# A hybrid attention and S5 block on one core: the GLU multiplies y itself, its buffers change places, sigmoids wait for the product alone, and the loads of turned u come in three parts

## The chip, the cores and the metric

The kernel runs on 1 core of one Trainium2 chip. The metric is the time of one execution in device microseconds (us); lower is better. Engines are named as in the profile: PE (TensorE), DVE (VectorE), ACT (ScalarE), POOL (GpSimd), SP (SyncE, which here only issues DMAs). ACT issues DMAs too, on a queue of its own; their issues are rows of "SPq" and "ACTq".

## The reference, cut to what matters

```python
# x: (1, 2048, 1024); one layer, float32
h = rms_norm(x, norm_mix)
q, k, v, u, g = split(h @ w_in)                        # u: 512 wide, g: two gates of 1024
branch_a = window_attention(q, k, v, sinks, bias) @ w_attn_branch
y = gelu(Re(C scan(A, B u)) + D u)                     # S5: 32 groups of 16 channels, 64 states each
branch_b = (y * sigmoid(y @ w_glu + b_glu)) @ w_ssm_branch
x = x + (sigmoid(g_A) * branch_a + sigmoid(g_B) * branch_b) @ w_out
x = x + conv_ffn(rms_norm(x, norm_ffn))                # 1024 -> 2 x 2816 -> 1024, depthwise conv of width 3
return rms_norm(x, norm_final)
```

## The kernel before

The 2048 tokens are worked on in two blocks (`blk`) of T = 1024. In each block PE goes through projections, attention with gate products between its pieces, the S5 recurrence with gate products between its pairs of groups, the GLU, the two branch products and merge, the output projection, and the ConvFFN. Everything is written out by hand in raw form: every engine has its own program, and semaphores set the order between engines. A float32 product is made of three matmuls on a high and a low part (fp32r) of each operand (`three`, L497 to L499); a half of a GLU or branch product (128 outputs, 512 tokens, four blocks of 128 inputs) is 12 matmuls of 512 columns.

**Weights.** They come in units of 512 KB. SP loads each into one of two buffers `w_raw` (L572), POOL makes the high part (L793, a cast) and the low part (L797, a subtraction) into one of two rings `w_hi`, `w_lo`; POOL may start on a unit when PE has used the one two units before, SP may load into `w_raw` when POOL is done with it. Units 6 and 11 to 25 are gates (two halves each), 26 and 27 the GLU, 28 to 35 the branches, and then those of the output projection (`wo`), which have eight buffers of their own.

**Turned u.** The S5 part wants u with eight consecutive tokens turned onto the partitions. ACT stores u to HBM (`useq`, semaphore `u_st`), and SP loads it back into `ssT` with eight DMAs of 256 KB, one for each token of a step (`load_steps`, L753; rows of 128 elements, 512 bytes). PE waits for all eight before the S5 loop, that is, after the attention.

**Gate halves.** ACT takes each gate product from PSUM into one of two buffers `junk` and stores it to HBM from its own DMA queue (`gate_out`, `gate_store`, L1046). It takes the next product of the same parity only when that store has landed. In the attention, one iteration of ACT is: 8 exponentials of a tile (L1129), `gate_out`, the high part of the attention output, the copy of the transposed probabilities; what comes next on ACT stands behind a `gate_out` that waits. In iteration 3 ACT also issues three loads of S5 tables (L1112).

**GLU.** y is turned back through HBM into `yT`. ACT makes `yT_hi` (`y_high`), DVE `yT_lo` = yT - yT_hi (`y_low`, L1616), in place of `yT` (both stand at 112 KiB). PE makes 8 half products. For each half n: ACT makes the sigmoid `glu_s`, DVE adds `yT_hi` and `yT_lo` again (L1674), multiplies by the sigmoid (L1676, `glu_y`), ACT makes the high part `ybr_hi`, and DVE the low part `ybr_lo` (L1681). `glu_s` and `glu_y` have two buffers each. The sigmoid of half n waits until `ybr_lo` of half n-2 is there (`ybr_ready`). PE works on the attention half of the first branch product meanwhile and then waits for all eight `ybr_lo`.

## Time and profile before

| | |
|---|---|
| time, median of 3 runs | 2474.99 us (2473.34 to 2483.62) |
| profiled execution | 2474.55 us, span in the trace 2472.8 us |
| PE busy | 2417.0 us, 98% of the span |
| DVE, ACT, POOL busy | 1737.5, 746.4, 855.5 us |
| TensorE clock granted, mean | 0.992 |

Busy time of PE is modelled from the start of its matmuls; a matmul of 512 columns shows 0.39 us, and the next one starts 0.23 us after it when PE runs through. PEclk is the granted clock as a share of full speed: 1.00 is 2.4 GHz, 0.50 is 1.2 GHz. Times in rows are in us from the start of the span, and idle time before an instruction stands in square brackets with what ended it.

### The profile page before, as it was taken

To read this page: it belongs to the slowest core of one execution; us is meant where nothing else is said; L and a number is where in the kernel's file an instruction comes from. 1 tells how busy PE (TensorE), PEld (TensorE's weight loads), DVE (VectorE), ACT (ScalarE), POOL (GpSimd) and SP (SyncE) were. 2 spreads that over 40 slices of the span, in tenths; PEclk is the share of its full clock that TensorE was granted. 3 is DMA by queue.
4 is the path that set the end of the run, shared out by engine and by line. 5 is a ranking of instruction groups with operands and counts; after the bars stand their busy time and mean duration, and the time that the engine had idled before them with its cause. 6 is when DMAs were issued, how large, how long until landed. Compare 5 with 4: busy or idle time off the path is not lost.

```text
span 2472.8 us, 33390 instructions
## 1 busy us (share of the span) xinstructions
PE 2417.0 (98%) x11578; PEld 1980.7 (80%) x11578; DVE 1737.5 (70%) x2585; ACT 746.4 (30%) x1431; POOL 855.5 (35%) x689
## 2 busy tenths in 40 slices
PE   7999999999999999999999999999999999999997
PEld 6887777888788888788878877778878888888886
DVE  6964564546899999989750346466378888888896
ACT  4145113212333333332221341132133333333222
POOL 2421222450455555623232222235213333334231
PEclk9999999999999999999999999999999999999999
DMA  6266553351334334698522536534312222218863
GB/s 206 77 182 108 175 170 120 133 194 71 102 126 156 135 131 133 216 371 290 183 88 90 104 119 188 158 105 156 148 60 80 91 85 76 78 75 289 311 230 136
DMA packets 178279, 367.35 MB, mean 149 GB/s; under 512 B 22344, under 2 KB 60008, under 8 KB 178168
## 3 DMA queue, kind: packets, MB, share of 16 engines
q1 hardware_dynamic: 135568, 278.23, 34.7%
q10 hardware_dynamic: 42600, 87.64, 10.3%
q8 instruction: 70, 1.15, 0.2%
q14 instruction: 41, 0.34, 0.0%
HBM read 277.20 MB, written 88.60 MB: 148 GB/s over the span
## 4 chain that ended last, share of the span: by engine, by line
PE 90%; DVE 5%; DMA 2%; ACT 2%; issue 1%; POOL 0%; ACTq 0%; SPq 0%; DVEq 0%; POOLq 0%
PE ps L497 28%; PE ps L499 28%; PE ps L498 28%; DMA gates<-junk 1%; PE ps L2220 1%; PE ps L2222 1%; PE ps L2202 1%; DVE ybr_lo L1681 1%; PE ps L2026 1%; PE ps L2074 0%; PE ps L2159 0%; DVE glu_y L1676 0%; ACT ybr_hi L909 0%; DVE z L1809 0%; DVE act_lo L1842 0%
## 5 line engine op out<-in xcount | busy, mean ns | idle before, releaser
L839 POOL CAST slot_hi<-pair_raw 128x512 fp32r<-128x512 f32 x220 | 201.7, 924 | 394.4 <-PE ps L499 305.5
L497 PE MATMUL ps<-act_hi,w_hi 128*128 128x512 f32 x832 | 332.1, 399 | 1.5 <-issue 1.5
L499 PE MATMUL ps<-act_hi,w_lo 128*128 128x512 f32 x832 | 325.4, 391 | 0.0
L498 PE MATMUL ps<-act_lo,w_hi 128*128 128x512 f32 x832 | 324.6, 390 | 0.0
L793 POOL CAST w_hi<-w_raw 128x1024 fp32r<-128x1024 f32 x72 | 80.6, 1119 | 678.4 <-PE ps L499 668.8
L497 PE MATMUL ps<-act_hi,slot_hi 128*128 128x512 f32 x704 | 274.4, 390 | 1.8 <-DVE pre L1795 1.5
L499 PE MATMUL ps<-act_hi,slot_lo 128*128 128x512 f32 x704 | 274.0, 389 | 0.0
L498 PE MATMUL ps<-act_lo,slot_hi 128*128 128x512 f32 x704 | 273.9, 389 | 0.0
L497 PE MATMUL ps<-act_hi 128*128 128x512 f32 x616 | 242.0, 393 | 3.2 <-DVE act_lo L1846 3.2
L498 PE MATMUL ps<-act_lo,act_hi 128*128 128x512 f32 x616 | 240.9, 391 | 0.0
L499 PE MATMUL ps<-act_hi,act_lo 128*128 128x512 f32 x616 | 240.8, 391 | 0.0
L899 POOL CAST act_hi<-step_w 128x512 fp32r<-128x512 f32 x154 | 136.2, 911 | 292.4 <-PE ps L499 280.9
L497 PE MATMUL ps<-tw_hi,slot_hi 128*128 128x512 f32 x528 | 206.3, 391 | 1.6 <-ACT part L909 1.4
L499 PE MATMUL ps<-tw_hi,slot_lo 128*128 128x512 f32 x528 | 205.5, 389 | 0.0
L498 PE MATMUL ps<-tw_lo,slot_hi 128*128 128x512 f32 x528 | 205.5, 389 | 0.0
L1742 DVE TENSOR_TENSOR slot_lo<-pair_raw,slot_hi 128x512 fp32r<-128x512 f32 x220 | 184.0, 838 | 13.8 <-POOL slot_hi L839 12.8
L797 POOL TENSOR_TENSOR w_lo<-w_raw,w_hi 128x1024 fp32r<-128x1024 f32 x72 | 186.3, 2588 | 9.9 <-DVE xin L1447 4.3
L839 POOL CAST slot_hi<-sums 128x512 fp32r<-128x512 f32 x84 | 118.8, 1414 | 202.8 <-DVE sums L1722 102.6
L497 PEld LDWEIGHTS ps<-act_hi,w_hi 128*128 128x128 f32 x832 | 156.8, 188 | 35.8 <-issue 3.6
L499 PEld LDWEIGHTS ps<-act_hi,w_lo 128*128 128x128 f32 x832 | 156.7, 188 | 34.0
L498 PEld LDWEIGHTS ps<-act_lo,w_hi 128*128 128x128 f32 x832 | 157.0, 189 | 30.9
L909 ACT ACTIVATE act_hi<-step_f 128x512 fp32r<-128x512 f32 x154 | 89.0, 623 | 268.7 <-PE ps L499 173.0
(325 smaller groups left out, 4953.2 us busy)
## 6 DMA issues: line engine op xcount, KB each, us to landing
w_raw<-in_wu SPq DMA_DIRECT2D x88, 512.0 KB, 3.4
pair_raw<-in_wu SPq DMA_DIRECT2D x88, 512.0 KB, 4.1
step_f<-ff SPq DMA_DIRECT2D x88, 512.0 KB, 5.2
ff<-z SPq DMA_DIRECT2D x44, 512.0 KB, 2.6
gates<-junk ACTq DMA_DIRECT2D x64, 256.0 KB, 2.1
sig<-gates ACTq DMA_DIRECT2D x32, 512.0 KB, 5.3
tbl_o<-tables ACTq DMA_DIRECT2D x32, 384.0 KB, 3.6
step_w<-in_wu SPq DMA_DIRECT2D x22, 512.0 KB, 6.8
```

What stands on the lines that cost most here:

```text
L497: nc.tensor.matmul(out, lh, rh, start=first, stop=False, skip_group_check=onto)
L498: nc.tensor.matmul(out, lh, rl, start=False, stop=False, skip_group_check=onto)
L499: return nc.tensor.matmul(out, ll, rh, start=False, stop=last, skip_group_check=onto)
L793: nc.gpsimd.tensor_copy(hi, w_raw[b][:, :]).then_inc(hi_made, 1)
L797: nc.gpsimd.tensor_tensor(lo, w_raw[b][:, :], f(hi), ALU.subtract).then_inc(w_ready, 1)
L839: nc.gpsimd.tensor_copy(slot_hi[j][:, :, :], src).then_inc(slot_half[KIND[j]], 1)
L899: nc.gpsimd.tensor_copy(d_hi[slot][part], weight_of(t, n)).then_inc(d_half, 1)
L909: ins = nc.scalar.activation(out, in_, kw.pop("func", ACT.Identity), **kw)
L1681: tt(by_step(ybr_lo, q), glu_y[b][:, :].rearrange("p (t n) -> p t n", t=4), f(by_step(ybr_hi, q)), ALU.subtract).then_inc(ybr_ready, 1)
L1742: tt(slot_lo[j][:, :, :], src, f(slot_hi[j][:, :, :]), ALU.subtract).then_inc(slot_ready[KIND[j]], 1)
L2026: return nc.tensor.transpose(ps[:, x_bank(blk, h, k), q * P:(q + 1) * P], src, ident[:, :])
L2202: ins = mm(ps[SS * g:SS * g + SS, s_bank[m % 2], ri * P:(ri + 1) * P], tbl_r[m % NR][:, TB_W + ri * P + SS * g:TB_W + ri * P + SS * g + SS ...
```

## The change

It has three parts.

**The GLU multiplies y itself.** `yT_lo` moves from 112 to 160 KiB, so that `yT` stays whole; the addition L1674 is gone, and the multiplication reads `yT`. `ybr_lo` moves from 160 to 112 KiB, over `yT`; before the first `ybr_lo` of a pair of halves is written, DVE waits until both products of this pair are made (`glu_yr`). At 160 to 176 KiB stand tables of the S5 loop, so all eight `y_low` now stand behind the loop, where four did before; two of the four `y_low` calls stood in the loop, at its steps 9 and 13. The buffers of `wo` are taken in another order.

**Sigmoids.** From n = 2 on, ACT's sigmoid of half n waits for the product of half n-2 (`glu_yr`) and not for its `ybr_lo`.

**Loads of turned u.** The eight DMAs are issued as three, three and two, with two weight units between the first and the second part and two between the second and the third.

```diff
@@ buffers
-        yT_lo = at("yT_lo", 112, [4, T], F32R)
+        yT_lo = at("yT_lo", 160, [4, T], F32R)
         ybr_hi = at("ybr_hi", 144, [4, T], F32R)
-        ybr_lo = at("ybr_lo", 160, [4, T], F32R)
+        ybr_lo = at("ybr_lo", 112, [4, T], F32R)
...
         wo = [(at(f"wo_hi{i}", a, [D], F32R), at(f"wo_lo{i}", a + 4, [D], F32R))
-              for i, a in enumerate((96, 104, 112, 120, 144, 152, 160, 168))]
+              for i, a in enumerate((96, 104, 160, 168, 112, 120, 144, 152))]
@@ SP
-                def load_steps():
+                def load_steps(lo, hi):
                     rows = A["useq"].rearrange("(g c) (t n) -> t c g n", c=SC, t=STEP)
                     sp.wait_ge(u_st, 16 * 4 * (blk + 1))
-                    for t in range(STEP):
+                    for t in range(lo, hi):
                         sp.dma_start(ssT[SC * t:SC * t + SC, :, :], rows[t]).then_inc(steps_in, 16)
-                load_weights(first, (U_GATE + 6) // 2)
-                load_steps()
+                if blk:
+                    load_weights(first, (U_GATE + 4) // 2)
+                load_steps(0, 3)
+                load_weights((U_GATE + 4) // 2, (U_GATE + 6) // 2)
...
-                load_weights((U_GATE + 6) // 2, (U_GATE + 14) // 2)
+                load_steps(3, 6)
+                load_weights((U_GATE + 6) // 2, (U_GATE + 8) // 2)
+                load_steps(6, STEP)
+                load_weights((U_GATE + 8) // 2, (U_GATE + 14) // 2)
                 load_y(0)
@@ ACT
                         if n >= 2:
-                            act.wait_ge(ybr_ready, blk * 8 + n - 1)
+                            act.wait_ge(glu_yr, blk * 8 + n - 1)
                         copy(glu_s[n % 2][:, :], ps[:, 2 + n % 4, :], glu_sig, 1, func=ACT.Sigmoid, bias=bglu[:, n // 2:n // 2 + 1])
@@ DVE
-                    if n in (9, 13):
-                        y_low((n - 9) // 4)
...
-                y_low(2)
-                y_low(3)
-
-                dve.wait_ge(y_ready, (blk + 1) * 8)
+                dve.wait_ge(y_done, (blk + 1) * PAIRS)
+                for kt in range(4):
+                    y_low(kt)
+
                 for n in range(9):
                     if n < 8:
...
                         if n >= 2:
                             dve.wait_ge(ybr_ready, blk * 8 + n - 1)
-                        link(tt(glu_y[b][:, :], f(yT_hi[:, m, cols]), f(yT_lo[:, m, cols]), ALU.add))
                         dve.wait_ge(glu_sig, blk * 8 + n + 1)
-                        tt(glu_y[b][:, :], glu_y[b][:, :], glu_s[b][:, :], ALU.mult).then_inc(glu_yr, 1)
+                        tt(glu_y[b][:, :], yT[:, m, cols], glu_s[b][:, :], ALU.mult).then_inc(glu_yr, 1)
                     if n >= 1:
                         q = n - 1
+                        b = q % 2
+                        if q % 2 == 0:
+                            dve.wait_ge(glu_yr, blk * 8 + min(q + 2, 8))
                         dve.wait_ge(glu_hi, blk * 8 + q + 1)
                         tt(by_step(ybr_lo, q), ...
```

On PE a wait for all eight `ybr_lo` stands before each of the two halves of the first S5 branch product, where it stood before the first alone.

**DVE, block 0, from the end of the S5 loop into the GLU** (`yT_lo` low parts of y, `glu_y` products, `ybr_lo` low parts of the branch's input). Before:

```order
L1616 TENSOR_TENSOR yT_lo<-yT,yT_hi 128x512 x4
L1674 TENSOR_TENSOR glu_y_99<-yT_hi,yT_lo 128x512
L1676 TENSOR_TENSOR glu_y_99<-glu_y_99,glu_s_97 128x512
L1674 TENSOR_TENSOR glu_y_100<-yT_hi,yT_lo 128x512
L1676 TENSOR_TENSOR glu_y_100<-glu_y_100,glu_s_98 128x512
L1681 TENSOR_TENSOR ybr_lo<-glu_y_99,ybr_hi 128x4x128
L1674 TENSOR_TENSOR glu_y_99<-yT_hi,yT_lo 128x512
L1676 TENSOR_TENSOR glu_y_99<-glu_y_99,glu_s_97 128x512
L1681 TENSOR_TENSOR ybr_lo<-glu_y_100,ybr_hi 128x4x128
```

The same place in the changed kernel:

```order
L1621 TENSOR_TENSOR yT_lo<-yT,yT_hi 128x512 x8
L1678 TENSOR_TENSOR glu_y_99<-yT,glu_s_97 128x512
L1678 TENSOR_TENSOR glu_y_100<-yT,glu_s_98 128x512
L1685 TENSOR_TENSOR ybr_lo<-glu_y_99,ybr_hi 128x4x128
L1678 TENSOR_TENSOR glu_y_99<-yT,glu_s_97 128x512
L1685 TENSOR_TENSOR ybr_lo<-glu_y_100,ybr_hi 128x4x128
```

Eight additions are gone, and eight `yT_lo` stand in a row instead of four.

**SP, block 0, from the last store of S5 tables to the first load of y** (`ssT` turned u, `w_raw` weight units). Before:

```order
L588 DMA tables<-set_kmat 16x16x16
L745 UNCONDITIONAL_BRANCH
L572 DMA w_raw_176<-in_wu 128x1024
L572 DMA w_raw_177<-in_wu 128x1024
L745 REGISTER_ALU
L745 COMPARE_AND_BRANCH
L753 DMA ssT<-useq 16x32x128 x8
```

In the changed kernel:

```order
L588 DMA tables<-set_kmat 16x16x16
L753 DMA ssT<-useq 16x32x128 x3
L745 UNCONDITIONAL_BRANCH
L572 DMA w_raw_176<-in_wu 128x1024
L572 DMA w_raw_177<-in_wu 128x1024
L745 REGISTER_ALU
L745 COMPARE_AND_BRANCH
L753 DMA ssT<-useq 16x32x128 x3
L745 UNCONDITIONAL_BRANCH
L572 DMA w_raw_176<-in_wu 128x1024
L572 DMA w_raw_177<-in_wu 128x1024
L745 REGISTER_ALU
L745 COMPARE_AND_BRANCH
L753 DMA ssT<-useq 16x32x128 x2
```

The first three loads of u now stand ahead of weight units 14 and 15, the next three right behind them, and the last two behind units 16 and 17. In block 1 the order is the same, with units 0 to 13 ahead of it.

## Rows read from the trace of the kernel before

**Rows 1.** The page, engine busy times and the chain by engine.
```profile
PE 2417.0 (98%) x11578; PEld 1980.7 (80%) x11578; DVE 1737.5 (70%) x2585; ACT 746.4 (30%) x1431; POOL 855.5 (35%) x689
...
PE 90%; DVE 5%; DMA 2%; ACT 2%; issue 1%; POOL 0%; ACTq 0%; SPq 0%; DVEq 0%; POOLq 0%
```

**Rows 2.** Stretches: us, busy (instructions) of PE, PEld, DVE, ACT, POOL; PEclk; DMA share; GB/s.
```profile
205.00:212.00 7.00, 4.99 (x42) 3.97 (x39) 1.60 (x3) 2.05 (x9) 0.00 (x0) 0.80 1.06 250
212.00:222.00 10.00, 10.00 (x52) 7.58 (x51) 5.93 (x13) 5.90 (x21) 2.45 (x2) 0.80 0.14 51
426.00:430.00 4.00, 3.96 (x9) 3.14 (x10) 1.12 (x1) 1.35 (x2) 0.00 (x0) 0.50 0.72 261
430.00:434.00 4.00, 4.00 (x17) 3.23 (x16) 0.00 (x0) 1.35 (x2) 0.00 (x0) 0.87 0.00 1
654.00:662.00 8.00, 6.48 (x29) 5.04 (x28) 7.76 (x9) 3.38 (x7) 5.07 (x6) 1.00 0.16 63
```

**Rows 3.** PE in order of time, block 0, GLU: start, us, [idle before <-releaser].
```profile
393.68 0.39 PE L497 MATMUL ps<-yT_hi,w_hi 128*128 128x512 f32 x1
...
415.44 0.39 PE L497 MATMUL ps<-attn_hi,w_hi 128*128 128x512 f32 x1
...
426.05 0.79 PE L497 MATMUL ps<-ybr_hi,w_hi 128*128 128x512 f32 x1 [5.01 <-DVE ybr_lo L1681]
```

**Rows 4.** PE in order of time, block 1, the same wait.
```profile
1641.67 0.80 PE L497 MATMUL ps<-ybr_hi,w_hi 128*128 128x512 f32 x1 [5.04 <-DVE ybr_lo L1681]
```

**Rows 5.** DVE in order of time, block 0, GLU.
```profile
381.43 1.29 DVE L1616 TENSOR_TENSOR yT_lo<-yT,yT_hi 128x512 fp32r<-128x512 f32 x2 [13.02 <-ACT yT_hi L909]
...
411.58 0.69 DVE L1676 TENSOR_TENSOR glu_y<-glu_y,glu_s 128x512 f32<-128x512 f32 x1 [0.16 <-ACT glu_s L909]
...
415.69 1.16 DVE L1681 TENSOR_TENSOR ybr_lo<-glu_y,ybr_hi 128x512 fp32r<-128x512 f32 x1 [0.32 <-ACT ybr_hi L909]
416.88 1.40 DVE L1674 TENSOR_TENSOR glu_y<-yT_hi,yT_lo 128x512 f32<-128x512 f32 x1
418.31 2.77 DVE L1676 TENSOR_TENSOR glu_y<-glu_y,glu_s 128x512 f32<-128x512 f32 x1
421.00 1.07 DVE L1681 TENSOR_TENSOR ybr_lo<-glu_y,ybr_hi 128x512 fp32r<-128x512 f32 x1
```

**Rows 6.** ACT in order of time, block 0, GLU.
```profile
416.94 0.69 ACT L909 ACTIVATE glu_s<-ps,bglu 128x512 f32<-128x512 f32 x1 [1.28 <-DVE ybr_lo L1681]
417.52 1.20 ACT L909 ACTIVATE ybr_hi<-glu_y 128x512 fp32r<-128x512 f32 x1
```

**Rows 7.** POOL in order of time, block 0, GLU.
```profile
415.80 1.93 POOL L793 CAST w_hi<-w_raw 128x1024 fp32r<-128x1024 f32 x1 [6.71 <-PE ps L499]
417.81 2.72 POOL L797 TENSOR_TENSOR w_lo<-w_raw,w_hi 128x1024 fp32r<-128x1024 f32 x1
```

**Rows 8.** The chain in order of time, block 0, attention: start, us, what.
```profile
186.00 13.41 DMA gates<-junk
...
201.49 1.10 ACTq L1112
```

**Rows 9.** PE in order of time, block 0, attention.
```profile
207.70 1.10 PE L2159 MATMUL ps<-ident,logit 128*128 128x128 f32 x8 [2.01 <-DVE logit L1594]
```

**Rows 10.** PE in order of time, block 1, attention.
```profile
1425.98 0.77 PE L2159 MATMUL ps<-ident,logit 128*128 128x128 f32 x5 [0.83 <-DVE logit L1594]
```

**Rows 11.** Waits of ACT, block 0, attention: us in total, times, longest.
```profile
ACT junk L909 <- DMA gates<-junk: 15.7, 3, 7.3
```

**Rows 12.** SP's DMA queue up to the late store, block 0.
```profile
181.84 0.86 SPq L572 DMA_DIRECT2D w_raw<-in_wu  x2
182.94 4.92 SPq L753 DMA_DIRECT2D ssT<-useq  x5
```

**Rows 13.** Tile ssT, block 1: DMA issues (ns, first and last start), time to landing.
```profile
L753 SPq DMA_DIRECT2D ssT<-useq x8: 330/1182/2417, 1401.7 to 1410.4; - x8
...
DMA to landing us min/median/max: 6.8/13.8/15.9
```

More of the change, by code:

```diff
@@ L1673, in _ @@
                             dve.wait_ge(ybr_ready, blk * 8 + n - 1)
-                        link(tt(glu_y[b][:, :], f(yT_hi[:, m, cols]), f(yT_lo[:, m, cols]), ALU.add))
                         dve.wait_ge(glu_sig, blk * 8 + n + 1)
-                        tt(glu_y[b][:, :], glu_y[b][:, :], glu_s[b][:, :], ALU.mult).then_inc(glu_yr, 1)
+                        tt(glu_y[b][:, :], yT[:, m, cols], glu_s[b][:, :], ALU.mult).then_inc(glu_yr, 1)
                     if n >= 1:
                         q = n - 1
-                        b, m, cols = q % 2, q // 2, slice((q % 2) * HALF, (q % 2 + 1) * HALF)
+                        b = q % 2
+                        if q % 2 == 0:
+                            dve.wait_ge(glu_yr, blk * 8 + min(q + 2, 8))
                         dve.wait_ge(glu_hi, blk * 8 + q + 1)
@@ L2244, in _ @@
                     for j in range(2):
-                        if m == 0 and j:
-                            pe.wait_ge(ybr_ready, (blk + 1) * 8)
                         for h in range(2):
+                            if m == 0 and j:
+                                pe.wait_ge(ybr_ready, (blk + 1) * 8)
                             ins = unit_half(4 * (m % 2) + 2 * j + h, m % 2, h, (attn_hi, ybr_hi)[j], (attn_lo, ybr_lo)[j], 4 * j, 4)
```

## The prediction

> **What bounds the kernel now.** I read the page first. PE is busy for 98% of the span and the chain that ended last runs over PE for 90% of it [rows 1]: only time in which PE stands still, or runs at the low clock, can be won. PE's idle time is 2472.8 - 2417.0 = 55.8 us in all. So I looked for PE's waits in the two places that the diff touches, and then for the clock behind them.
>
> In the GLU, PE makes eight half products from 393.68 to 415.44, 2.72 us each, works on the attention half of the first branch product, and stands still for 5.01 us until the last `ybr_lo`, at 426.05 [rows 3]. Block 1 has the same wait, 5.04 us [rows 4]. Behind it the granted clock is 0.50, that is 1.2 GHz, for the 4 us from 426 and at a mean of 0.87 over the next 4 us, which makes 4 + 1.04 = 5.0 us at half speed [rows 2]: 2.5 us of work lost beyond the wait itself. For block 1 I take the same.
>
> In the attention of block 0, a gate store issued at 186.00 lands after 13.41 us [rows 8]; ACT wants its buffer 7.3 us before that [rows 11], and everything behind it on ACT is late. PE waits 2.01 us for the probabilities at 207.70 [rows 9]. The mean clock is 0.80 over the 7 us from 205 and 0.80 over the 10 us from 212 [rows 2], so 2.8 + 4.0 = 6.8 us at half speed, 3.4 us lost. Block 1 has a wait of 0.83 us there [rows 10].
>
> **The GLU, step by step.** Why is the last `ybr_lo` late? The products would allow a half each 2.72 us. Before, the sigmoid of half n waited for `ybr_lo` of half n-2, so sigmoid, product, high part and low part stood in a ring. When POOL works on a weight unit, DVE's share stretches: the addition at 416.88 takes 1.40 and the product at 418.31 takes 2.77 us, where the same product takes 0.69 at 411.58 [rows 5]; POOL's cast and subtraction run at 415.80 and 417.81 [rows 7]. This happens twice in a block, and the ring hands each delay on. Now the sigmoid waits only for PE and for a product two halves back, and DVE has one operation of 0.69 us less per half. Per half DVE needs 0.69 + 1.2 = 1.9 and ACT 0.69 + 1.20 = 1.9 us [rows 5, 6], under PE's 2.72. So the chain should run at PE's pace, and only the last two halves show.
>
> The last product ends just before 415.80, since POOL's cast waits for it too [rows 7]. By my reckoning with the durations above: `ybr_lo` of half 5 from about 414.8 to 415.9; sigmoid of half 7 from 415.7 to 416.4; POOL's cast, behind that `ybr_lo`, to about 416.9; the product of half 7 from then to 417.6; high part of half 6 to 417.5 and of half 7 to 418.9; POOL's subtraction, asked for at 417.0 and so ahead of the next `ybr_lo`, from 417.6 to 419.9 (its 2.72 less the 0.4 in which it was held up); `ybr_lo` of half 6 to 421.0, of half 7 to 422.1. PE starts at 422.2, not at 426.05: 3.85 us per block, and a wait of 422.2 - 421.04 = 1.2 us remains. Another wait of about this size, 1.52 us near 655 (8.00 - 6.48 busy), leaves the clock at 1.00 [rows 2], so I take the 2.5 us as won too. Per block 3.85 + 2.5 = 6.35, for two blocks **12.7 us**. Bounds: with no POOL work in the way the wait vanishes, 5.0 + 2.5 = 7.5 per block, 15.0; with the clock falling all the same 3.85 per block, 7.7.
>
> The remaining wait is where a rule speaks against the change. The rows show it first: the product at 418.31 ends at 421.08, 0.55 us after POOL's subtraction (417.81 + 2.72 = 420.53) [rows 5, 7], as if it had not begun before. The Trainium skill (SBUF — State Buffer, Who interferes with whom) says that a DVE instruction with two inputs in SBUF contends with a GpSimd instruction that reads SBUF, and that the one issued second is blocked entirely. By that rule the new product, which still has two SBUF inputs, is blocked as the old one was, and the wait of 1.2 us stays; if instead both only slowed down, the last `ybr_lo` would come near 421 and the sum would be 15 instead of 12.7.
>
> **The moved low parts.** All eight `yT_lo` now follow the S5 loop; two make 1.29 us [rows 5], so the four that leave the loop are 2.6 us. DVE is idle for 13.02 us before 381.43 [rows 5], in which they fit, and the last two wait for y to come back from HBM as before. Cost nothing; without that cover 2.6 us per block. The wait for the pair's two products, on DVE itself, comes after an instruction that has just been issued there; the first `ybr_lo` already waits for `ybr_hi`. It is at nothing, with 0.16 us per pair at most, by the wait for the own result in [rows 5]. Other buffers for `wo` and PE's doubled wait move nothing: the second wait is for a number already reached.
>
> **The loads of u.** In block 1 a part takes (1410.4 + 15.9 - 1401.7 - 6.8) / 7 = 2.5 us when the parts are queued (first landing to last) [rows 13]. The gate store of block 0 lands 13.41 us after issue, five parts (12.7 us) and a bit [rows 8], and five parts had been handed over or begun by then (182.94 + 4.92) [rows 12]: a store lands when what was issued ahead of it has gone through. So what counts is what SP has issued by the time ACT stores.
>
> Block 0: the two weight units were issued at 181.84, right ahead of the parts [rows 12]. Now three parts go first, then the units, then three parts without any wait between. At 186.00 about the same is in front of the store, and it lands near 199.4 again. But two of eight parts, 5 us, are gone behind it, and with them the 1.10 us for which ACT's exponentials waited on the issue of a table load into a full queue [rows 8]. PE's wait becomes 2.01 - 1.1 = 0.9 us, like the 0.83 of block 1, whose mean clock the page does not show falling. Gain 1.1 + 3.4 = **4.5 us**; bounds 0 (wait and clock as before) and 5.4 (all gone).
>
> Block 1: SP can load unit 15 only when POOL is done with unit 13, an iteration after unit 14, so the first two parts are truly apart. A store has three parts in front of it instead of five, lands about 5 us earlier, and the 0.83 us go: **0.8 us**, bounds 0 and 0.8. The first part comes an iteration earlier; the last two parts still come iterations before PE asks for them. Behind `u_st` on SP stand weight units 14 and 15 now; POOL can take unit 14 only when PE has used unit 12, so a delay of 3 x 2.5 = 7.5 us lies within its slack.
>
> **Sum.** 12.7 + 4.5 + 0.8 = 18.0 us. The profiled execution took 2474.55, 1.8 above its span and 0.4 below the median of the runs shown: 2474.55 - 18.0 = 2456.5, and against the median 2457.0 us, which I forecast (0.7% faster). About 0.5%, 12.4 us, is what a measurement of this kernel can tell from no change: the border is at 2462.6.
>
> **Rivals.**
> - *No wait remains in the GLU.* DVE's last two low parts slip in ahead of POOL, or POOL's subtraction comes later. For it: the order at 417.6 is a matter of 0.1 us. Time 2457.0 - 2.3 = 2454.7. Chance 0.12.
> - *The clock falls behind the remaining wait.* The row at 655 speaks against it, but at 207.70 a wait of 2.01 us was enough [rows 2, 9], and 1.2 lies between. One block 2459.5, both 2462.0. Chance 0.14.
> - *Block 0's attention keeps its wait.* Three parts, two units, three parts back to back are nearly the old burst. Then 4.5 is missing: 2461.5. Chance 0.15; together with a clock that falls, 2466.5, 0.05.
> - *The GLU change does not do what it says*: the chain was bound by POOL, and the low part of half 7 still ends near 426, because each of the twelve operations in between yields to POOL. Against it: ACT stood idle 1.28 us before the sigmoid at 416.94, and what ended that was `ybr_lo` [rows 6], the very wait that is taken out. 2457.0 + 12.7 = 2469.7. Chance 0.04.
> - *Slower*: each of the three parts holds up a gate store, in each block. Before, one store per block is that late. If every part makes a store land 13.4 us after issue, as in [rows 8], and PE pays 2.01 + 3.4 = 5.4 us each time, six such places cost 32.4 against the 6.2 of before: 26 more, less 12.7 won in the GLU, 2475.0 + 26.2 - 12.7 = 2488.5. Its point: a store may take 13.4 - 7.3 = 6.1 us before ACT is late, and PE has 7.3 + 1.1 - 2.01 = 6.4 us of slack behind ACT [rows 8, 9, 11], so it costs from 12.5 us on; three parts and a weight unit are below 10. Chance 0.03.
>
> **How the numbers follow.** The forecast as written has 0.47. Range 2452 to 2467: below it lies only both upper bounds and more (15.0 + 6.2 = 21.2, 2453.8, with a microsecond or two for the spread of runs), above it the last two rivals. Faster by over 0.5%: forecast, first two rivals and nearly all of the third, 0.83. Within 0.5%: part of the third, third with second, the fourth, 0.13. Slower 0.04.
>
> **What would show it.** PE's idle before the first product with `ybr_hi` at 1.2 us instead of 5.01 in both blocks, with PEclk 1.00 behind it; sigmoids 2.7 us apart, waiting for PE; product and `ybr_lo` stretched where POOL subtracts. In the attention, a gate store that still takes 13 us in block 0 and about 8 in block 1, and a wait of PE under 1 us in place of 2.01, with no 0.80 in PEclk. It is wrong if PE waits elsewhere: for `y_ready` at the head of the GLU, for `steps_in` ahead of the S5 loop, or for probabilities in another iteration.

## The result and the profile after

The changed kernel takes **2454.79 us** (median of 4 runs, 2454.64 to 2455.12); the kernel before, beside it on the same chip, 2474.16 (4 runs, 2470.70 to 2483.62). The ratio is 0.9923, 95% interval 0.9905 to 0.9941: 19.4 us or 0.8% faster. The forecast was 2457.0 us, range 2452 to 2467. The profiled execution took 2454.71 us with a span of 2452.9 us, 19.9 less than before, and the mean granted clock rose from 0.992 to 0.998.

The page, engine busy times and the chain by engine; they answer to [rows 1]:

```profile
PE 2408.1 (98%) x11578; PEld 1973.6 (80%) x11578; DVE 1726.3 (70%) x2569; ACT 747.8 (30%) x1431; POOL 855.0 (35%) x689
...
PE 92%; DVE 4%; DMA 1%; issue 1%; ACT 1%; SPq 0%; POOL 0%; DVEq 0%; POOLq 0%; ACTq 0%
```

PE's busy time fell by 8.9 us with the same number of matmuls; they ran less at the low clock, as the stretches below show. The other 11.0 us of the span are idle time of PE that is gone (55.8 to 44.8).

PE in order of time. Block 0: the attention's transposed probabilities, which waited at 207.70 [rows 9], the first matmul of the GLU, and the first product with `ybr_hi` [rows 3]. The last two rows are block 1's, an iteration of the attention and the same product.

```profile
205.54 1.09 PE L2163 MATMUL ps<-ident,logit 128*128 128x128 f32 x8
...
388.36 0.39 PE L497 MATMUL ps<-yT_hi,w_hi 128*128 128x512 f32 x1
...
416.43 0.50 PE L497 MATMUL ps<-ybr_hi,w_hi 128*128 128x512 f32 x1 [0.71 <-DVE ybr_lo L1685]
...
1413.05 0.66 PE L2163 MATMUL ps<-ident,logit 128*128 128x128 f32 x4
...
1623.98 0.50 PE L497 MATMUL ps<-ybr_hi,w_hi 128*128 128x512 f32 x1 [0.75 <-DVE ybr_lo L1685]
```

Block 1's attention and GLU had 0.83 and 5.04 us of wait before [rows 4, 10]. Set beside the rows of before, they say where the time went. The GLU of block 0 begins 393.68 - 388.36 = 5.3 us earlier: all of that was won in the attention. Its product with `ybr_hi` is 426.05 - 416.43 = 9.6 us earlier, 4.3 more, which is 5.01 - 0.71. In block 1 it is 1641.67 - 1623.98 = 17.7 us earlier. The stretches that answer to [rows 2], with the same columns, and one in the ConvFFN:

```profile
205.00:212.00 7.00, 7.00 (x55) 5.65 (x52) 4.21 (x12) 5.02 (x20) 0.00 (x0) 1.00 0.12 44
212.00:222.00 10.00, 10.00 (x68) 7.83 (x67) 5.88 (x13) 5.40 (x20) 3.39 (x2) 1.00 0.41 97
416.00:420.00 4.00, 3.57 (x16) 2.96 (x17) 1.51 (x2) 0.00 (x0) 0.00 (x0) 1.00 0.84 280
420.00:424.00 4.00, 4.00 (x19) 3.34 (x18) 1.69 (x2) 2.12 (x2) 1.50 (x2) 1.00 0.22 87
1038.00:1046.00 8.00, 8.00 (x30) 6.41 (x29) 8.00 (x12) 1.05 (x2) 2.56 (x2) 0.79 0.55 178
```

The clock stays at 1.00 (2.4 GHz) where it was 0.80, 0.80, 0.50 and 0.87. The last row is the one place in the middle of the program where it still falls.

**DVE in the GLU, block 0** (answers to [rows 5]):

```profile
372.21 2.50 DVE L1621 TENSOR_TENSOR yT_lo<-yT,yT_hi 128x512 fp32r<-128x512 f32 x4 [9.11 <-PE ps L2226]
...
385.30 1.29 DVE L1621 TENSOR_TENSOR yT_lo<-yT,yT_hi 128x512 fp32r<-128x512 f32 x2 [8.09 <-ACT yT_hi L914]
...
401.32 3.21 DVE L1685 TENSOR_TENSOR ybr_lo<-glu_y,ybr_hi 128x512 fp32r<-128x512 f32 x1
404.57 0.69 DVE L1678 TENSOR_TENSOR glu_y<-yT,glu_s 128x512 f32<-128x512 f32 x1
405.18 1.19 DVE L1685 TENSOR_TENSOR ybr_lo<-glu_y,ybr_hi 128x512 fp32r<-128x512 f32 x1
...
409.42 1.18 DVE L1685 TENSOR_TENSOR ybr_lo<-glu_y,ybr_hi 128x512 fp32r<-128x512 f32 x1 [0.34 <-ACT ybr_hi L914]
411.11 0.95 DVE L1678 TENSOR_TENSOR glu_y<-yT,glu_s 128x512 f32<-128x512 f32 x1 [0.51 <-ACT glu_s L914]
412.21 4.17 DVE L1685 TENSOR_TENSOR ybr_lo<-glu_y,ybr_hi 128x512 fp32r<-128x512 f32 x2
```

**POOL, the same stretch** (answers to [rows 7]):

```profile
400.78 2.73 POOL L802 TENSOR_TENSOR w_lo<-w_raw,w_hi 128x1024 fp32r<-128x1024 f32 x1
...
411.60 2.75 POOL L802 TENSOR_TENSOR w_lo<-w_raw,w_hi 128x1024 fp32r<-128x1024 f32 x1
```

The stretched `ybr_lo` at 401.32 ends at 404.53 instead of after 1.2 us, and POOL's subtraction beside it at 403.51. Now the delay is not handed on: DVE runs without a gap from 404.57, two operations of 0.69 and 1.19 us per half against PE's 2.72, and by 409.42 it is waiting for ACT again. In the last stretch two low parts that take 1.2 us each take 4.17: the first of them 3.18 us, to 415.39, which is 1.04 us behind the end of POOL's subtraction. PE's remaining 0.71 us of wait comes from there. DVE's idle time in front of the low parts of y (9.11 and 8.09 us) shows that four more of them cost nothing.

**ACT, the same stretch** (answers to [rows 6]):

```profile
404.88 0.69 ACT L914 ACTIVATE glu_s<-ps,bglu 128x512 f32<-128x512 f32 x1 [0.94 <-PE ps L499]
...
407.60 0.69 ACT L914 ACTIVATE glu_s<-ps,bglu 128x512 f32<-128x512 f32 x1 [0.95 <-PE ps L499]
```

Sigmoids stand 2.72 us apart, PE's pace, and what they wait for is PE and no longer `ybr_lo`.

**The attention.** SP's queue in block 0 (answers to [rows 12]), then the landing of the gate store of 185.9 (answers to [rows 8]), then ACT's waits, in us in total, times and longest (answers to [rows 11]):

```profile
181.53 1.52 SPq L753 DMA_DIRECT2D ssT<-useq  x3
183.17 0.89 SPq L572 DMA_DIRECT2D w_raw<-in_wu  x2
184.31 2.63 SPq L753 DMA_DIRECT2D ssT<-useq  x3
...
218.28 0.85 SPq L753 DMA_DIRECT2D ssT<-useq  x2
```

```profile
L1051 ACTq DMA_DIRECT2D gates<-junk x1: 326/326/326, 185.9 to 185.9; - x1
...
DMA to landing us min/median/max: 10.5/10.5/10.5
```

```profile
ACT junk L914 <- DMA gates<-junk: 7.8, 2, 4.4
```

The store lands after 10.5 us and not after 13.41, so ACT's longest wait for it is 4.4 us instead of 7.3, and PE has nothing to wait for. Six loads and two weight units are handed over in a row, at least as much as in the burst of before up to that time (two units and, by 187.9, five loads [rows 12]), only in another order.

### The profile page after: what moved, and what is told of

Read it like the earlier page. It is cut to its first block, busy times and chain, and to the rows that moved or that the text cites. A ratio compares the mean times of both kernels' runs of the same rounds, so it can differ in the third digit from the quotient of the medians.

```text
span 2452.9 us, 33368 instructions
## 1 busy us (share of the span) xinstructions
PE 2408.1 (98%) x11578; PEld 1973.6 (80%) x11578; DVE 1726.3 (70%) x2569; ACT 747.8 (30%) x1431; POOL 855.0 (35%) x689
## 3 DMA queue, kind: packets, MB, share of 16 engines
q8 instruction: 70, 1.15, 0.2%
## 4 chain that ended last, share of the span: by engine, by line
PE 92%; DVE 4%; DMA 1%; issue 1%; ACT 1%; SPq 0%; POOL 0%; DVEq 0%; POOLq 0%; ACTq 0%
PE ps L497 29%; PE ps L499 28%; PE ps L498 28%; PE ps L2224 1%; PE ps L2226 1%; PE ps L2206 1%; PE ps L2174 1%; PE ps L2163 1%; PE ps L2030 1%; DVE act_lo L1846 1%; DMA step_w<-tw 1%; PE ps L2078 0%; DVE act_lo L1850 0%; PE ps L2154 0%; DVE z L1813 0%
## 5 line engine op out<-in xcount | busy, mean ns | idle before, releaser
L1746 DVE TENSOR_TENSOR slot_lo<-pair_raw,slot_hi 128x512 fp32r<-128x512 f32 x220 | 184.0, 838 | 13.4 <-POOL slot_hi L844 12.4
```

Source lines behind the costliest of these rows:

```text
L1746: tt(slot_lo[j][:, :, :], src, f(slot_hi[j][:, :, :]), ALU.subtract).then_inc(slot_ready[KIND[j]], 1)
```

## The experiments

The expectations name theories by letter. A is the prediction's account where nothing else is said; B is the rival of that run; C and D, in the last two, are two accounts of when a store on ACT's queue lands beside SP's loads: after a certain number of SP's DMAs (C), or when all bytes handed over ahead of it have gone through (D).

**1. The loads in parts alone.** The kernel before, with nothing but the new `load_steps`:

```diff
-                load_weights(first, (U_GATE + 6) // 2)
-                load_steps()
+                if blk:
+                    load_weights(first, (U_GATE + 4) // 2)
+                load_steps(0, 3)
+                load_weights((U_GATE + 4) // 2, (U_GATE + 6) // 2)
...
-                load_weights((U_GATE + 6) // 2, (U_GATE + 14) // 2)
+                load_steps(3, 6)
+                load_weights((U_GATE + 6) // 2, (U_GATE + 8) // 2)
+                load_steps(6, STEP)
+                load_weights((U_GATE + 8) // 2, (U_GATE + 14) // 2)
```

> The kernel before with the loads of turned u in three parts, and nothing else of the change. Theory A (the gains are won place by place and add up): the comparison of the two traces gives 5.3 us in block 0's attention and 1.35 us in block 1's, so about 6.6 us less than before, near 2467.5 us; PE's waits of 5.0 us in the GLU stay, and no wait over 0.5 us is left in either attention. Rival B (the stores are quicker in the changed kernel only because other work around them moved): within 2 us of before, with a gate store of 13 us in block 0.

Measured 2467.70 us (10 runs, 2466.79 to 2469.48) against 2474.41 for before, ratio 0.9964 (0.9950 to 0.9978): 6.7 us. The store of 186 lands after 10.7 us, PE has no wait in either attention, and both waits of the GLU stand (5.05 and 5.02 us).

**2. The GLU and the sigmoids alone.** The changed kernel with the eight loads in one burst at their old place.

```diff
-                if blk:
-                    load_weights(first, (U_GATE + 4) // 2)
-                load_steps(0, 3)
-                load_weights((U_GATE + 4) // 2, (U_GATE + 6) // 2)
+                load_weights(first, (U_GATE + 6) // 2)
+                load_steps(0, STEP)
...
-                load_steps(3, 6)
-                load_weights((U_GATE + 6) // 2, (U_GATE + 8) // 2)
-                load_steps(6, STEP)
-                load_weights((U_GATE + 8) // 2, (U_GATE + 14) // 2)
+                load_weights((U_GATE + 6) // 2, (U_GATE + 14) // 2)
```

> The changed kernel with the eight loads of turned u in one piece, at their old place. Theory A: the 13.0 us of the two GLUs stay and the 6.6 us of the attention are given back: 2461.4 us; PE waits 0.7 us ahead of the first S5 branch product and 2.0 us for the probabilities of block 0 with the low clock behind it. Rival B (the low clock in the attention came from somewhere else): about 2456 us.

Measured 2461.67 us (9 runs, 2456.32 to 2468.17), ratio 0.9949 (0.9929 to 0.9969): 12.7 us. The GLU's waits are 0.73 and 0.72 us; the store takes 13.8 us, and PE waits for probabilities again, 1.42 us and in the next iteration 4.30:

```profile
207.04 1.09 PE L2158 MATMUL ps<-ident,logit 128*128 128x128 f32 x8 [1.42 <-DVE logit L1594]
...
220.76 1.97 PE L2158 MATMUL ps<-ident,logit 128*128 128x128 f32 x8 [4.30 <-DVE logit L1594]
```

The two halves of the change add up in the medians: 6.7 + 12.7 = 19.4 us, the whole. Their intervals are some 3 and 5 us wide to either side, so this is no close test, and place by place it is not what was expected. The profiled execution of this kernel (2465.67 us, 4 above its median) loses some 10 us to the changed kernel in block 0's attention, not 5.3, and nothing in block 1's: although the burst is there, with stores that land after 11.0 and 9.7 us, PE has no wait.

**3. The old wait of the sigmoid in the changed kernel.**

```diff
-                            act.wait_ge(glu_yr, blk * 8 + n - 1)
+                            act.wait_ge(ybr_ready, blk * 8 + n - 1)
```

> The changed kernel, but the sigmoid of half n waits for the low part of half n-2, as before. Theory A (the ring sigmoid, high part of the half before, low part, next sigmoid set the pace; the addition was hidden behind the sigmoid): steps of 0.69 + 1.1 + 1.18 + about 0.1 = 3.07 us again, PE waits 3 to 5 us in each block and the clock falls behind it: 2454.8 + 2 x (3 to 4.3 + 2.4) = 2465.6 to 2468.2 us. Rival B (what is won comes from the addition that is gone and from what POOL no longer stretches): steps near 2.7 us and under 2 us of waiting, below 2458 us.

Measured 2466.11 us (10 runs, 2465.23 to 2467.13), ratio 0.9964 (0.9948 to 0.9981). PE, ahead of the product with `ybr_hi`, and ACT's sigmoids before it:

```profile
419.51 0.80 PE L497 MATMUL ps<-ybr_hi,w_hi 128*128 128x512 f32 x1 [4.39 <-DVE ybr_lo L1685]
```

```profile
404.46 0.69 ACT L914 ACTIVATE glu_s<-ps,bglu 128x512 f32<-128x512 f32 x1 [3.08 <-DVE ybr_lo L1685]
...
407.58 0.69 ACT L914 ACTIVATE glu_s<-ps,bglu 128x512 f32<-128x512 f32 x1 [1.32 <-DVE ybr_lo L1685]
...
410.71 0.69 ACT L914 ACTIVATE glu_s<-ps,bglu 128x512 f32<-128x512 f32 x1 [1.36 <-DVE ybr_lo L1685]
...
415.55 0.69 ACT L914 ACTIVATE glu_s<-ps,bglu 128x512 f32<-128x512 f32 x1 [3.05 <-DVE ybr_lo L1685]
```

This is theory A, with both waits at 4.39 us. With the ring closed again, a lighter DVE hardly helps: after POOL's first unit the sigmoids follow at 3.12 and 3.13 us, slower than PE's 2.72, so what was lost is never caught up, and the second unit adds to it.

**4. The new wait of the sigmoid in the kernel before**, with its addition left in.

```diff
-                            act.wait_ge(ybr_ready, blk * 8 + n - 1)
+                            act.wait_ge(glu_yr, blk * 8 + n - 1)
```

> The kernel before with one edit: the sigmoid of half n waits for the product of half n-2. DVE still adds y, 0.69 + 0.69 + 1.18 us and about 0.3 of waits for its own results per half, 2.86, a little over PE's 2.72, and POOL stretches an addition and a product twice per block. Theory A: the wait shrinks from 5.0 to 2 to 3.5 us per block; the clock falls all the same if the wait is 2 us or more: 2474.2 - 2 x (1.5 to 3) = 2468.2 to 2471.2 us, and some 5 us less if the clock holds. Rival B (the wait alone does nothing without the addition gone): within 1 us of before.

Measured 2472.59 us (10 runs, 2465.19 to 2483.90), ratio 0.9983 (0.9961 to 1.0005): no change that can be told. The waits of the GLU are 3.78 and 3.81 us, over the 2 to 3.5 of theory A and under the 5 us that stay by rival B, and the clock still falls behind them. DVE shows why:

```profile
409.07 1.49 DVE L1674 TENSOR_TENSOR glu_y<-yT_hi,yT_lo 128x512 f32<-128x512 f32 x1
410.59 2.78 DVE L1676 TENSOR_TENSOR glu_y<-glu_y,glu_s 128x512 f32<-128x512 f32 x1
413.29 1.17 DVE L1681 TENSOR_TENSOR ybr_lo<-glu_y,ybr_hi 128x512 fp32r<-128x512 f32 x1
414.50 0.69 DVE L1674 TENSOR_TENSOR glu_y<-yT_hi,yT_lo 128x512 f32<-128x512 f32 x1
415.22 0.69 DVE L1676 TENSOR_TENSOR glu_y<-glu_y,glu_s 128x512 f32<-128x512 f32 x1
...
421.64 3.38 DVE L1681 TENSOR_TENSOR ybr_lo<-glu_y,ybr_hi 128x512 fp32r<-128x512 f32 x1
```

The ring is open, but three operations take 0.69 + 0.69 + 1.17 = 2.55 us per half, so DVE wins back only some 0.2 us per half on PE and is still late when the second unit of POOL stretches it again. Either edit alone leaves 4.4 or 3.8 us of wait; the two together leave 0.7. Block 0's attention has the program of before here, and yet its waits are others, 0.66 us at 206.31 and then this one, with the clock at a mean of 0.57 over 218 to 228:

```profile
219.50 1.97 PE L2159 MATMUL ps<-ident,logit 128*128 128x128 f32 x8 [3.77 <-DVE logit L1594]
```

That costs this execution 4 us more in the attention than the profiled one of before.

**5. POOL's second unit later.** The changed kernel, in which POOL takes the unit after the first branch unit only when all eight `ybr_lo` are there. Its loop is cut off at this unit:

```diff
-                with pool.Fori(1 if blk == 0 else 0, U_OUT // 2) as i:
+                with pool.Fori(1 if blk == 0 else 0, U_AB // 2) as i:
                     for b in range(2):
                         ring(i * 2 + (r0 + b), i + h0, i * 2 + (u0 + b), b)
+                for u in range(U_AB, U_OUT):
+                    if u == U_AB + 1:
+                        pool.wait_ge(ybr_ready, (blk + 1) * 8)
+                    ring(r0 + u, h0 + u // 2, u0 + u, u % 2)
```

> The changed kernel, but POOL makes the parts of the second branch unit only when all eight low parts are there, so that it reads no SBUF beside the last low parts. Theory A (the wait of 0.7 us is what POOL's subtraction adds to the low part of half 6, which takes about 3 us there instead of 1.18): the last two low parts take 2.1 us instead of 4.17, PE does not wait ahead of the first S5 branch product, the unit is ready at about +3.6 us, before PE wants it at +5.4: 2 x 0.7 = 1.4 us less than the changed kernel, 2453.4 us. Rival B (the last low parts are late for the steps ahead of them): the same wait, and the same time within 0.3 us; or the unit comes too late and PE waits there instead, 2455 to 2458 us.

Measured **2452.35 us** (6 runs, 2451.82 to 2453.05) against 2474.19 for before, ratio 0.9919 (0.9906 to 0.9933). Its slowest run is 1.6 us below the changed kernel's fastest (2454.64), and both stand beside equal medians of before (2474.16 and 2474.19); but they were not run side by side. DVE, then POOL:

```profile
411.88 2.26 DVE L1689 TENSOR_TENSOR ybr_lo<-glu_y,ybr_hi 128x512 fp32r<-128x512 f32 x2 [0.39 <-ACT ybr_hi L918]
```

```profile
414.33 1.04 POOL L798 CAST w_hi<-w_raw 128x1024 fp32r<-128x1024 f32 x1 [11.20 <-DVE ybr_lo L1689]
415.45 2.41 POOL L802 TENSOR_TENSOR w_lo<-w_raw,w_hi 128x1024 fp32r<-128x1024 f32 x1
```

The last two `ybr_lo` take 2.26 us instead of 4.17, and PE goes from its attention half at 415.02 to the product with `ybr_hi` at 415.25 without a wait. POOL has the unit ready at 417.9. The gain is 2.4 us where 1.4 was expected. Set instruction by instruction beside the changed kernel it is 1.01 and 1.05 us at the two products: the expectation counted the idle time of 0.7 alone, but the matmul behind the wait starts 1.10 us after the one before it instead of 0.23, and the next one 0.1 us late. The edit delays POOL's cast as well as its subtraction; what the run shows is that POOL's work on this unit makes the wait. This is the fastest kernel of the study.

**6. The parts later**: three loads behind units 14 and 15, three behind 16 and 17, two behind 18 and 19.

```diff
-                if blk:
-                    load_weights(first, (U_GATE + 4) // 2)
+                load_weights(first, (U_GATE + 6) // 2)
                 load_steps(0, 3)
-                load_weights((U_GATE + 4) // 2, (U_GATE + 6) // 2)
...
-                load_steps(3, 6)
                 load_weights((U_GATE + 6) // 2, (U_GATE + 8) // 2)
+                load_steps(3, 6)
+                load_weights((U_GATE + 8) // 2, (U_GATE + 10) // 2)
                 load_steps(6, STEP)
-                load_weights((U_GATE + 8) // 2, (U_GATE + 14) // 2)
+                load_weights((U_GATE + 10) // 2, (U_GATE + 14) // 2)
```

> The changed kernel, with the three parts one pair of weight units later (units 14 and 15 first, then three loads; units 16 and 17, three; 18 and 19, two). Theory A (a store takes as long as what was issued ahead of it and right behind it on SP's queue): block 0's store lands after some 8 us instead of 10.6, block 1's as now; PE has no wait there already: the same time within 1 us. Rival B: the last part now comes too late for the S5 loop, or collides with the loads of S5 tables, and PE waits at the loop's head: 2456 to 2462 us.

Measured 2484.69 us (4 runs, 2484.14 to 2486.64), ratio 1.0052 (1.0034 to 1.0070): slower than before, and 30 us slower than the changed kernel. Rival B had the place right and the price, at most 7 us, much too low. SP's queue and PE at the head of the S5 loop:

```profile
218.34 1.85 SPq L753 DMA_DIRECT2D ssT<-useq  x3
236.19 15.26 SPq L572 DMA_DIRECT2D w_raw<-in_wu  x2
251.66 0.85 SPq L753 DMA_DIRECT2D ssT<-useq  x2
```

```profile
261.20 1.12 PE L2205 MATMUL ps<-ssT,tbl_r 128*64 128x128 f32 x8 [12.82 <-issue]
```

SP can load unit 19 only when POOL gives its buffer free, at 251.0; the last two loads of u stand behind it, while PE has finished the attention at 248.4. PE stands still for 12.82 us, 13.15 in block 1, and runs at a mean clock of 0.69 for the 8 us behind. The store of 186, with only three loads behind the two units, lands after 9.9 us, which wins nothing more.

**7. All eight loads at the early place**, ahead of units 14 and 15.

```diff
-                load_steps(0, 3)
+                load_steps(0, STEP)
...
-                load_steps(3, 6)
-                load_weights((U_GATE + 6) // 2, (U_GATE + 8) // 2)
-                load_steps(6, STEP)
-                load_weights((U_GATE + 8) // 2, (U_GATE + 14) // 2)
+                load_weights((U_GATE + 6) // 2, (U_GATE + 14) // 2)
```

> The changed kernel, with all eight loads at the place of its first part, ahead of units 14 and 15. It tells the place from the splitting. Theory A (what counts is the number of loads in a burst beside a store): in block 0 the burst is as long as before and a store takes 13 us, PE waits 1 to 2 us with the low clock behind it, 5.3 us back; in block 1 the burst is one iteration earlier and costs 0.8 to 5 us: 2460 to 2465 us. Rival B (the earlier place alone wins it): the time of the changed kernel within 1 us.

Measured 2469.16 us (10 runs, 2464.98 to 2473.11), ratio 0.9982 (0.9971 to 0.9994). The store takes 14.3 us, and PE waits 3.29 us in block 0 and 3.19 us in block 1, more than theory A gave, whose range ended at 2465. The early place alone is worse than the old one: experiment 2 had a ratio of 0.9949, at most 0.9969.

**8. Six and two**: units 14 and 15, six loads, units 16 and 17, two loads.

```diff
-                if blk:
-                    load_weights(first, (U_GATE + 4) // 2)
-                load_steps(0, 3)
-                load_weights((U_GATE + 4) // 2, (U_GATE + 6) // 2)
+                load_weights(first, (U_GATE + 6) // 2)
+                load_steps(0, 6)
...
-                load_steps(3, 6)
                 load_weights((U_GATE + 6) // 2, (U_GATE + 8) // 2)
```

> The changed kernel, with six loads at the old place behind units 14 and 15 and the last two behind units 16 and 17. In block 0 the burst has the same six loads and two units as in the changed kernel, in another order. Theory A (only the two loads that are gone from the burst count in block 0): its store takes 10 to 11 us as in the changed kernel and PE does not wait; in block 1 the burst has six loads instead of three, its store some 11 us, PE waits at most 0.3 us: 2454.8 to 2456 us. Rival B (the units between the loads let the store through): the store takes 13 us in block 0, PE waits, 2458 to 2461 us.

Measured 2459.27 us (4 runs, 2456.36 to 2462.39), ratio 0.9951 (0.9932 to 0.9970). In block 0 SP hands over the same eight DMAs as the changed kernel, the two units first instead of in the middle, and the store takes 13.6 us and not 10.5:

```profile
L1048 ACTq DMA_DIRECT2D gates<-junk x1: 326/326/326, 186.0 to 186.0; - x1
...
DMA to landing us min/median/max: 13.6/13.6/13.6
```

PE waits 1.91 us for it, and this time the clock stays at 1.00:

```profile
205.00:212.00 7.00, 5.09 (x46) 4.00 (x43) 3.84 (x9) 5.20 (x21) 0.00 (x0) 1.00 0.32 121
```

Theory A, which gave 10 to 11 us, falls with this run, and rival B holds in landing, wait and time. What differs from the changed kernel up to the store is the order alone.

**9. Halved loads**: the kernel of experiment 2 with each load of u cut in two DMAs of 128 KB (PE waits for sixteen).

```diff
-                        sp.dma_start(ssT[SC * t:SC * t + SC, :, :], rows[t]).then_inc(steps_in, 16)
+                        for g in range(0, SG, SG // 2):
+                            sp.dma_start(ssT[SC * t:SC * t + SC, g:g + SG // 2, :], rows[t][:, g:g + SG // 2]).then_inc(steps_in, 16)
...
-                pe.wait_ge(steps_in, 16 * STEP * (blk + 1))
+                pe.wait_ge(steps_in, 16 * 2 * STEP * (blk + 1))
```

> Eight loads of turned u in one burst at the old place (as in e2_glu_alone), each cut into two DMAs of 128 KB over half of the groups: 16 DMAs, the same bytes and rows. In e2_glu_alone the store at 185.9 took 13.8 us and PE waited 1.42 us behind it. Theory C (a gate store gets one turn of service for each DMA of SP's queue and needs about five turns, so that it matters how long SP's DMAs are): the store lands after some 7 to 9 us, PE does not wait for probabilities, and the time is that of the changed kernel or 1 us above it, 2455 to 2457 us. Theory D (a store lands when the bytes ahead of it have landed, however they are cut): 13 to 14 us, PE waits 1 to 2 us as in e2_glu_alone, 2460 to 2463 us.

Measured 2454.94 us (4 runs, 2454.49 to 2463.08), ratio 0.9931 (0.9904 to 0.9958). The burst has the same place and the same bytes, and the store lands after 10.3 us instead of 13.8; PE has no wait in the attention. The time is the one of theory C, but the landing is neither its 7 to 9 us nor the 13 to 14 of theory D.

**10. Three and five**: three loads, units 14 and 15, the other five in one.

```diff
-                load_steps(3, 6)
-                load_weights((U_GATE + 6) // 2, (U_GATE + 8) // 2)
-                load_steps(6, STEP)
-                load_weights((U_GATE + 8) // 2, (U_GATE + 14) // 2)
+                load_steps(3, STEP)
+                load_weights((U_GATE + 6) // 2, (U_GATE + 14) // 2)
```

> The changed kernel, but the last two loads of turned u join the second part: three, units 14 and 15, five. In block 0 this is the burst of before with the two units behind the third load instead of ahead of the first. Theory C (turns: two of the store's five turns fall on weight units, which are quicker than loads of u): the store at 185.9 lands after 10 to 11 us as in the changed kernel (e8_six_then_two, with the units in front, took 13.6), and PE waits less than 0.7 us in block 0. Theory D (what is ahead or beside it in bytes): 13 us as in e8_six_then_two, and a wait of 1.5 to 2 us. In block 1 both expect a store of 11 to 13 us behind five loads and at most 0.9 us of waiting. Time 2455 to 2457 us by C, 2458 to 2462 us by D.

Measured 2456.04 us (4 runs, 2454.09 to 2457.52) against 2475.88, ratio 0.9924 (0.9902 to 0.9946). The store lands after 10.8 us although all eight loads are handed over in a row:

```profile
L1049 ACTq DMA_DIRECT2D gates<-junk x1: 326/326/326, 186.0 to 186.0; - x1
...
DMA to landing us min/median/max: 10.8/10.8/10.8
```

That is theory C's landing. In block 0 the units between the loads do nearly all of it; the third part adds little. In block 1 a wait of 0.70 us is left at 1414.22, which the changed kernel doesn't have.

## Why the prediction was right, and where it was not

**The GLU: right in mechanism and size.** 4.3 us of wait went per block (5.01 to 0.71, 5.04 to 0.75). Set instruction by instruction beside that of before, PE's program gains another 2.3 us (block 0) and 2.1 us (block 1) in the 7 us behind the wait, where the clock was low: 13.0 us where 12.7 was forecast. That the ring handed on each of POOL's two delays, and that both edits are needed to break it, is shown by experiments 3 and 4. The prediction named both edits, but not that neither does much alone: DVE must not only be let go, it must have time to catch up between POOL's two units (1.9 of 2.72 us per half against 2.55).

**The remaining wait: right in cause, somewhat too large.** Forecast 1.2 us, measured 0.71 and 0.75. With the 5.32 us added by which this execution is ahead, the sigmoid of half 7 (415.64) and POOL's cast (to 416.84) came as reckoned. The product of half 7 and the subtraction ended about 0.2 us sooner each (at 417.38 and 419.67 instead of 417.6 and 419.9), and the two low parts took another 0.2 less, to 421.70 instead of 422.1. That POOL's work on the unit is the cause is shown by experiment 5; that it is the subtraction is read from the times. The low parts at 401.32 and 412.21 end 1.02 and 1.04 us behind the subtraction that they were issued beside; undisturbed they take 1.15 to 1.2, as if they had begun only then. Had both engines gone at half speed, an estimate from that duration gives 2.4 us for such a low part, where 3.21 and 3.18 were measured. This agrees with the rule of the Trainium skill (SBUF — State Buffer, Who interferes with whom) that the prediction weighed: the one issued second is blocked, not slowed.

**The clock behind the remaining wait: right.** 1.00 behind 0.71 and 0.75 us. The rival in which it falls gives 2459.5 and more. The time alone could not tell the forecast from the first rival, no wait in the GLU: its 2454.7 is the measured time to 0.1 us, and yet the wait is there. It is luck that they meet; the microseconds came from the attention.

**The low parts of y and the other edits at nothing: right.** DVE idles 9.11 and 8.09 us in front of them, and PE shows no new wait at the head of the GLU.

**The attention of block 0: the gain is right within a microsecond, one step is wrong.** Forecast 4.5, measured 5.3: all of the wait of 2.01 us and of the 3.4 us of clock, within 0.1, which is about the upper bound of 5.4. All of this is two executions; experiments 2 and 4 show that the burst costs more in others. The step that failed is "At 186.00 about the same is in front of the store, and it lands near 199.4 again." The store of 185.9 landed after 10.5 us, at 196.4. So the wait went wholly, where 0.9 us was to stay. The step before it, that a store lands when what was issued ahead has gone through, was drawn from one row and doesn't hold: experiments 8 and 10 move the same DMAs past each other and get 13.6 and 10.8 us, and experiment 9 changes only how they are cut and gets 10.3. The slack that the prediction worked out for its slowest rival, that PE pays from a landing of about 12.5 us on, does fit block 0: at 10.8 us and less PE waits 0.35 us at most, at 13.2 and more it waits in each run. The landings of this one store:

| in front, from 181.5 on | store of 186 lands after |
|---|---|
| units, eight loads (before; experiments 2, 4) | 13.4; 13.8, 13.2 us |
| eight loads, units (7) | 14.3 |
| units, six loads (8) | 13.6 |
| three loads, units, five loads (10) | 10.8 |
| three loads, units, three loads (changed; 1, 3, 5) | 10.5; 10.7, 10.3, 10.6 |
| units, three loads (6) | 9.9 |
| units, sixteen halved loads (9) | 10.3 |

What is shown is that order and cut of SP's DMAs decide, at equal bytes. How they do is open. Theory C, a turn for each of SP's DMAs, gave experiments 9 and 10 the right direction; theory D, bytes, fails in both. The packets of the two queues (q1 is SP's, q10 ACT's; packets, MB, share of the 16 engines) say more. From 186 to 194, before, where ACT's queue has no row, and then in the changed kernel:

```profile
q1 hardware_dynamic: 1752, 0.96, 124.8%
```

```profile
q1 hardware_dynamic: 1114, 1.46, 104.8%
q10 hardware_dynamic: 138, 0.25, 8.3%
```

So the store does not go slowly beside the loads: it starts late, and then goes fast. Its first packet moves 8.7 us after its issue before the change, 6.8 in the changed kernel, 5.7 in experiment 9 and 11.0 in experiment 7; its last one starts 1.9 to 4.3 us behind the first in all runs. Between issue and first packet SP's queue moves 3.8, 3.0, 5.0 (halves) and 4.3 of its DMAs, or 1.0, 1.3, 0.7 and 1.1 MB: neither a fixed number of DMAs nor of bytes fits. In the runs without units between the loads the store starts when all but a part of one load (0.1 to 0.7 of it) of what was handed over ahead of it has moved, nearly as the prediction's step has it. In the changed kernel it overtakes two loads that were handed over ahead of it, behind the units. Why it does so there, no run shows.

**The attention of block 1: right in the number, the cause only in part shown.** 0.8 forecast, all of the wait of 0.83 us gone; PE gained 1.35 us there, of which a second wait of 0.40 us at 1435.82 is a part. The stores land after at most 8.0 us instead of 13.4, as forecast (about 5 us earlier). But PE has no wait in block 1 in the profiles of experiments 2 and 4 either, which keep the burst and have stores of 11.0 and 11.1 us. So the wait of before comes and goes with the same loads, and what the parts are worth here is less sure than the two profiles make it look.

**Sum.** 13.0 + 5.3 + 1.35 = 19.65, and 0.2 net from the ConvFFN: its low stretch of clock near 1050 is shorter (1.3 us won), and a wait of 0.76 us for `xres` at 1089.19 is new. That makes the 19.9 us of the spans. The forecast's 18.0 misses 1.4 to 1.9 of it, most of it (0.8 and 0.55) in the two attentions.

**The rival on the slower side** did not come, but loads in parts can make the kernel slower: in experiment 6 one of them hurts not by holding up a store but by being issued too late. The changed kernel is two weight units away from that: its last part is issued at 218.28 and wanted at 248.5, and two units later it is issued at 251.66.

## What to carry to other kernels

Where an engine waits at the end of a chain of others, look for a ring in it (a step that waits for a later step of an earlier turn): it hands on each disturbance in full, and opening it pays only if the slowest engine in it then has time to catch up, so give it less work in the same change. Where a small store on one queue lands late beside a burst on another, try quicker DMAs between the slow ones (here units of 512 KB, some 2.1 us each by their packets in the changed kernel, against 2.5 for a load of 256 KB [rows 13]) or cut the slow ones, before moving the whole burst, and see when the last of them is wanted. When a wait in front of PE goes, count the clock behind it too; here the clock was 8.9 of the 19.9 us.

## What was not expected of the hardware

- A store of 256 KB that lands after 2.0 us when nothing is beside it took 9.9 to 14.3 us beside loads on another engine's queue, and the figure followed the order of these loads (13.6 against 10.8) and their cut (13.8 against 10.3), not their bytes.
- The clock does not follow the length of a wait alone: 2.01 us in the kernel before brought 6.8 us at half speed [rows 2, 9], and 1.91 us at the same place in experiment 8 none.
- The spread of runs goes with the burst of loads. Kernels with all eight in one burst vary by 18 us (before, 30 runs), 12 (experiment 2), 19 (4) and 8 (7); those with three parts by 0.5 us (changed, 4 runs), 2.7 (1), 1.9 (3) and 1.2 (5), although 1 and 3 keep waits of 4.4 to 5 us in the GLU. Experiments 8 to 10, four runs each, lie between with 6.0, 8.6 and 3.4. The three profiles with the units and then the eight loads show one way to it: PE's waits in block 0's attention are 2.01 us in one, 0.66 and 3.77 in another, 1.42 and 4.30 in the third, each with its own stretch of low clock.
